# Attention of the samples joined with the preparation of the heads, ahead of the heads

## The reference, cut to what matters

```python
def _dsa_block(qb, qib, wb, posb, k_all, v_all, ki_all, topk, slopes):
    ...
    top_val, top_idx = lax.top_k(score, topk)
    k_sel = k_all[bidx, top_idx]
    v_sel = v_all[bidx, top_idx]
    logits = jnp.einsum('bqhgd,bqshd->bqhgs', qb, k_sel).astype(jnp.float32) * (HEAD_DIM_A ** -0.5)
    dist = jnp.abs(posb[None, :, None] - top_idx).astype(jnp.float32)
    logits = logits - slopes[None, None, :, :, None] * dist[:, :, None, None, :]
    ...
    p = jax.nn.softmax(logits, axis=-1).astype(v_sel.dtype)
    return jnp.einsum('bqhgs,bqshd->bqhgd', p, v_sel)
...
    k_all = jnp.concatenate([past_k.astype(x.dtype), k_a], axis=1)
    v_all = jnp.concatenate([past_v.astype(x.dtype), v_a], axis=1)
    ...
    o_a = o_a * jax.nn.silu(z_a)
```

## Time and profile before

| | us |
|---|---|
| median of 3 runs (lowest, highest) | 3160.65 (3158.35, 3172.86) |
| the profiled execution | 3176.13 |
| its span, first to last instruction | 3174.0 |
| PE busy | 2804.9 (88%) |
| DVE, ACT, POOL busy | 1156.2, 948.0, 819.6 |
| `prepare_heads`, first DMA issue to the next stage's first | 1797.16 to 1826.54 |
| `attend_samples`, the same | 2644.05 to 2727.75 |
| mean granted clock of PE, as a share of 2.4 GHz | 0.921 |

### The profile page before, as it was taken

One profiled execution on the slowest core, in us unless ns is written; L12 is line 12 of the kernel. 1 busy time (PEld: TensorE's weight loads), 2 busy tenths in 40 slices (PEclk: granted clock), 3 DMA queues, 4 the chain that ended last, 5 costly groups with the idle time before them and its releaser, 6 DMA issues. The chain is left out here.

```text
span 3174.0 us, 40095 instructions
## 1 busy us (share of the span) xinstructions
PE 2804.9 (88%) x15405; PEld 2516.8 (79%) x15429; DVE 1156.2 (36%) x2044; ACT 948.0 (30%) x1657; POOL 819.6 (26%) x713
## 2 busy tenths in 40 slices
PE   4999899999999999999999747787788785799997
PEld 3999599798998989999999736666677663587875
DVE  7000100752909044070600154566665552204142
ACT  5111111313112121121211245555556542222221
POOL 6222022111111211211122212323312320355553
PEclk6999699999999989999999877988998995699998
DMA  3222222122121212212222321222122113446453
GB/s 127 64 72 63 42 62 66 55 65 65 59 75 45 68 49 65 81 49 67 66 65 70 110 84 40 78 78 70 28 67 70 56 42 85 169 153 228 159 179 126
DMA packets 301721, 259.04 MB, mean 82 GB/s; under 512 B 88232, under 2 KB 252176, under 8 KB 299152
## 3 DMA queue, kind: packets, MB, share of 16 engines
q1 hardware_dynamic: 291564, 212.35, 23.0%
q10 hardware_dynamic: 10048, 45.27, 3.5%
HBM read 192.25 MB, written 65.33 MB: 81 GB/s over the span
## 5 line engine op out<-in xcount | busy, mean ns | idle before, releaser
L394 PE MATMUL bank<-hH,wL 128*128 128x384 f32 (+1 forms) x2928 | 981.5, 335 | 14.9 <-POOL wL L311 14.9
L395 PE MATMUL bank<-hL,wH 128*128 128x384 f32 (+1 forms) x2928 | 979.9, 335 | 0.0
L396 PE MATMUL bank<-hH,wH 128*128 128x384 f32 (+1 forms) x2928 | 979.7, 335 | 0.0
L311 POOL TENSOR_TENSOR wL<-raw,wH 128x512 fp32r<-128x512 f32 x244 | 314.2, 1288 | 1388.7 <-ACT wH L328 1388.7
L394 PEld LDWEIGHTS bank<-hH,wL 128*128 128x128 f32 (+1 forms) x2928 | 549.8, 188 | 19.2 <-issue 18.5
L395 PEld LDWEIGHTS bank<-hL,wH 128*128 128x128 f32 (+1 forms) x2928 | 549.9, 188 | 0.8
L396 PEld LDWEIGHTS bank<-hH,wH 128*128 128x128 f32 (+1 forms) x2928 | 549.8, 188 | 0.7
L328 ACT ACTIVATE wH<-raw 128x512 fp32r<-128x512 f32 x244 | 154.2, 632 | 1018.9 <-PE bank L396 963.1
L1906 POOL TENSOR_TENSOR owL<-oraw,owH 128x2048 fp32r<-128x2048 f32 x48 | 225.5, 4700 | 267.7 <-ACT owH L1926 267.7
L506 DVE TENSOR_SCALAR score<-relued,w_idx 128x512 f32<-128x512 f32 (+3 forms) x10 | 7.8, 778 | 683.4 <-ACT relued L353 683.0
L1965 PE MATMUL ob<-owH,mL 128*128 128x512 f32 x576 | 227.0, 394 | 28.6 <-POOL owL L1906 28.6
(11 more groups left out here) (302 smaller groups left out, 3521.0 us busy)
## 6 DMA issues: line engine op xcount, KB each, us to landing
raw<-in_w_in SPq DMA_DIRECT2D x240, 256.0 KB, 2.8
oraw<-in_w_out SPq DMA_DIRECT2D x48, 1024.0 KB, 5.1
proj_scratch<-ptbuf ACTq DMA_DIRECT2D x60, 576.0 KB, 2.8
xc<-proj_scratch SPq DMA_DIRECT2D x8, 1536.0 KB, 7.6
mraw<-mix_scratch SPq DMA_DIRECT2D x12, 768.0 KB, 6.1
x<-in_x_prompt SPq DMA_DIRECT2D x8, 1024.0 KB, 4.9
out_y_prompt<-yv ACTq DMA_DIRECT2D x8, 1024.0 KB, 4.4
ox<-in_x_prompt SPq DMA_DIRECT2D x8, 768.0 KB, 6.8
```

The costliest lines, as they stand in the source:

```text
L311: pool.tensor_tensor(wL[c % 2][:, :, :], raw[c][:, :, :], wH[c % 2][:, :, :].bitcast(F32), ALU.subtract).then_inc(low_ready, 1)
L394: pe.matmul(o, low, hH[:, kk, tok], start=first, stop=False)
L395: pe.matmul(o, high, hL[:, kk, tok], start=False, stop=False)
L396: last = pe.matmul(o, high, hH[:, kk, tok], start=False, stop=end)
```

## The change

`attend_samples` is gone as a stage; its programs are written into `prepare_heads`, now `prepare_and_attend`, ahead of the heads. The instructions of the tables and of the units are the old ones. What differs:

- PSUM: one bank `gate_bank` holds gates and sums; four banks `turn_bank` serve in turn the convolution rows, the nine tiles of `kvT` and the eight turns of cached keys, and then two of them the logits and two the turned probabilities; two banks hold the products; one `out_bank` holds the turned results, so that a result may be turned only when the gate of the unit before is done.
- The tiles of `kvT` are turned from the last (the samples') to the first.
- SP: behind `kvT` come all loads of the samples, `zs` now ahead of the values; then, when the nine tiles are copied, the two stores of the samples' new keys and values, a wait for both, the load `vnew`, the two stores of the prompt, and only then the heads' keys, the masks and `gnw`.
- PE: the cached keys are turned behind `kvT` and ahead of the sums of the gates. ACT and DVE do the samples' work behind all work of the preparation.

```diff
-def prepare_heads(nc, io, scratch, keep, ident, done_with):
+def prepare_and_attend(nc, io, scratch, keep, ident, done_with):
...
+        gate_bank = ctx.enter_context(nc.psum_tensor("gate_bank", [P, 512], F32))
+        turn_bank = [ctx.enter_context(nc.psum_tensor(f"turn_bank{i}", [P, 512], F32)) for i in range(4)]
+        vbank = [ctx.enter_context(nc.psum_tensor(f"value_bank{i}", [P, P], F32)) for i in range(2)]
+        obank = ctx.enter_context(nc.psum_tensor("out_bank", [P, P], F32))
+        lbank, tbank = turn_bank[0:2], turn_bank[2:4]
...
                 sp.dma_start(kvT[:, :, :], proj[C_K:C_Z, :].rearrange("(n p) t -> p n t", p=P)).then_inc(kv_loaded, 16)
+                sp.dma_start(kn[:, :, :, :], io["cache_k"]...).then_inc(cache_loaded, 16)
+                for k in range(KV):
+                    for b in range(DEC_B):
...
+                        sp.dma_start(qs[:, k, b, :, :], ...).then_inc(q_loaded, 16)
+                    sp.dma_start(kT[:, k, :, PAST:], ...).then_inc(q_loaded, 16)
+                sp.dma_start(smask[:, :], scratch["sample_mask"]).then_inc(q_loaded, 16)
+                sp.dma_start(zs[:, :, :], ...).then_inc(z_loaded, 16)
+                sp.dma_start(vn[:, :, :, :], io["cache_v"]...).then_inc(v_loaded, 16)
+                sp.wait_ge(moved, TILES)
...
+                    sp.dma_start(io[name + "_sample"]..., flat[:, NT, c:c + 2 * P]).then_inc(stored, 16)
+                sp.wait_ge(stored, 32)
+                sp.dma_start(vnew[:, :, :], io["new_v_sample"]...).then_inc(v_loaded, 16)
...
+                    sp.dma_start(io[name + "_prompt"]..., flat[:, 0:NT, c:c + 2 * P]).then_inc(stored, 16)
                 sp.dma_start(K["kT"][:, :, :], ...).then_inc(loaded, 16)
...
+                def bank_free(n):
+                    if n >= CACHE_AT + 4:
+                        pe.wait_ge(s_moved, n - CACHE_AT - 3)
+                    elif n >= KV_AT + 4:
+                        pe.wait_ge(moved, n - KV_AT - 3)
+                    elif n >= 4:
+                        pe.wait_ge(rows_out, n - 3)
...
-                for t in range(TILES):
-                    if t >= 4:
-                        pe.wait_ge(moved, t - 3)
+                for t in range(TILES - 1, -1, -1):
+                    done = TILES - 1 - t
+                    bank_free(KV_AT + done)
...
                 def turn_out(i):
                     pe.wait_ge(on_ready, i + 1)
-                    if i >= 2:
-                        pe.wait_ge(mixed, i - 1)
-                    pe.transpose(bank[6 + i % 2][:, 0:P], oN[i % 2][:, :], ident[:, :]).then_inc(on_turned, 1)
+                    if i:
+                        pe.wait_ge(mixed, i)
+                    pe.transpose(obank[:, :], oN[i % 2][:, :], ident[:, :]).then_inc(on_turned, 1)
...
-            prepare_heads(nc, io, scratch, keep, ident, done_with)
+            prepare_and_attend(nc, io, scratch, keep, ident, done_with)
             run_heads(nc, io, scratch, keep, ident)
-            attend_samples(nc, io, scratch, keep, ident)
         project_out(nc, io, scratch)
```

More of the change, by code:

```diff
@@ L528, in sem @@
             return ctx.enter_context(nc.semaphore(name))
-        proj = scratch["proj"]
+        proj, mix = scratch["proj"], scratch["mix"]
         kvT = sbt("kvT", [P, 4, TOK])
@@ L549, in prepare_heads @@
             sem, ["gate_loaded", "kv_loaded", "rows_loaded", "rows_turned", "rows_out", "summed", "drained"])
[L550 to L553, removed]
+        G, K = keep["gates"], keep
+        segcol = K["segcol"]
@@ new lines, in prepare_and_attend @@
+        PAIRS = DEC_B // 2
+        UNITS = KV * PAIRS
+        SLICES = ((0, P), (P, P), (2 * P, DEC_T))
+        qs = sbt("qs", [P, KV, DEC_B, GROUP, DEC_T])
+        zs = sbt("zs", [P, H, P])
+        kn = sbt("kn", [P, DEC_B, 2, KV * P])
+        kT = sbt("kTs", [P, KV, DEC_B, LS])
+        vn = sbt("vns", [P, DEC_B, 2, KV * P])
+        vnew = sbt("vnew", [DEC_T, DEC_B, KV * P])
+        smask = sbt("smask", [P, LS], BF16)
+        rsel = sbt("rsel", [P, PAIRS, P], BF16)
+        row = sbt("row", [P, LS], mybir.dt.int32)
@@ L654, in _, with logits @@
                 pe.matmul(segp, ones[:, :], gseg[:, :, :], start=True, stop=True).then_inc(summed, 1)
+                pe.wait_ge(q_loaded, 16 * (KV * (DEC_B + 1) + 1))
+                pe.wait_ge(s_tabled, 2)
+                pe.wait_ge(s_moved, UNITS)
+                def logits(i):
+                    k, pair = divmod(i, PAIRS)
+                    if i >= 2:
+                        pe.wait_ge(lg_ready, i - 1)
+                    o = lbank[i % 2]
+                    pe.matmul(o[:, 0:LS], rsel[:, pair, :], smask[:, :], start=True, stop=False, skip_group_check=True)
+                    for j in range(2):
+                        b = 2 * pair + j
+                        last = pe.matmul(o[j * 64:(j + 1) * 64, 0:LS], qs[:, k, b, :, :].rearrange("p g t -> p (g t)"), kT[:, k, b, :],
+                                         start=False, stop=True, skip_group_check=True)
+                    last.then_inc(lg_done, 1)
@@ new lines, in turn_out @@
+                def turn_out(i):
+                    pe.wait_ge(on_ready, i + 1)
+                    if i:
+                        pe.wait_ge(mixed, i)
+                    pe.transpose(obank[:, :], oN[i % 2][:, :], ident[:, :]).then_inc(on_turned, 1)
+                logits(0)
+                for i in range(UNITS):
+                    k, pair = divmod(i, PAIRS)
+                    if i + 1 < UNITS:
+                        logits(i + 1)
+                    pe.wait_ge(exp_ready, i + 1)
+                    if i >= 2:
+                        pe.wait_ge(p_ready, i - 1)
+                    for n, (c, w) in enumerate(SLICES):
+                        last = pe.transpose(tbank[i % 2][0:w, n * P:(n + 1) * P], lg[i % 2][:, c:c + w], ident[:, :])
+                    last.then_inc(p_turned, 1)
+                    if i:
+                        turn_out(i - 1)
+                    pe.wait_ge(p_ready, i + 1)
+                    if i == 0:
+                        pe.wait_ge(v_loaded, 32)
+                    if i >= 2:
+                        pe.wait_ge(on_ready, i - 1)
+                    for j in range(2):
+                        b = 2 * pair + j
+                        for n, (c, w) in enumerate(SLICES):
+                            v = vn[:, b, n, k * P:(k + 1) * P] if n < 2 else vnew[:, b, k * P:(k + 1) * P]
+                            last = pe.matmul(vbank[i % 2][j * 64:(j + 1) * 64, :], pT[i % 2][0:w, n, j * 64:(j + 1) * 64], v,
+                                             start=(n == 0), stop=(n == 2))
+                    last.then_inc(pv_done, 1)
@@ L656, in _ @@
+                turn_out(UNITS - 1)
             @block.scalar
@@ L666, in _ @@
                     act.wait_ge(rows_turned, half + 1)
[L667 to L670, removed]
+                    nc.scalar.activation(K["cw"][:, half * 3 * H // 2:(half + 1) * 3 * H // 2, :], turn_bank[half][:, 0:3 * H // 2 * ROWS].rearrange("p (n c) -> p n c", c=ROWS), ACT.Copy).then_inc(rows_out, 1)
+                for t in range(TILES - 1, -1, -1):
+                    done = TILES - 1 - t
+                    act.wait_ge(turned, done + 2)
+                    nc.scalar.activation(kvN[:, t, :, :], turn_bank[(KV_AT + done) % 4][:, :].rearrange("p (n c) -> p n c", n=4), ACT.Copy).then_inc(moved, 1)
+                for i in range(UNITS):
+                    k, pair = divmod(i, PAIRS)
+                    act.wait_ge(s_turned, i + 1)
+                    nc.scalar.activation(kT[:, k, 2 * pair:2 * pair + 2, 0:PAST], turn_bank[(CACHE_AT + i) % 4][:, :].rearrange("d (b s) -> d b s", b=2), ACT.Copy).then_inc(s_moved, 1)
                 act.wait_ge(stepped, 16)
@@ new lines, in _ @@
+                sample_chain(V.tensor_copy(col[:, 3:4], pcol[:, :]))
+                sample_chain(V.tensor_tensor(col[:, 1:2], col[:, 3:4], col[:, 0:1], ALU.subtract))
+                sample_chain(V.tensor_copy(rowf[:, :], row[:, :]))
+                sample_chain(V.tensor_scalar(rowf[:, :], rowf[:, :], col[:, 1:2], None, ALU.add))
+                sample_chain(V.scalar_tensor_tensor(out=rowf[:, :], in0=rowf[:, :], scalar=-1.0, in1=rowf[:, :], op0=ALU.mult, op1=ALU.min))
+                for k in range(KV):
+                    sample_chain(V.tensor_scalar(alibi[:, k, :], rowf[:, :], col[:, 2:3], 2.0 ** (-8.0 * k * GROUP / H), ALU.mult, ALU.mult))
@@ new lines, in _ @@
+                add(0)
+                dve.wait_ge(silued, 1)
+                for i in range(UNITS):
+                    if i + 1 < UNITS:
+                        add(i + 1)
+                    if i:
+                        gate(i - 1)
+                    dve.wait_ge(exp_ready, i + 1)
+                    V.reciprocal(am[:, i, 3:4], am[:, i, 2:3]).then_inc(inv_ready, 1)
+                    dve.wait_ge(inv_ready, i + 1)
+                    dve.wait_ge(pv_done, i + 1)
```

(2 more changed lines are left out.)

287 lines of the change are left out of this document (94 added, 193 removed).

## The result

The kernel after took 3155.04 us in the median of 20 runs (3135.77 to 3164.25). Beside it, on the same chip, the kernel before took 3175.07 us in 20 runs (3158.35 to 3184.45). The ratio is 0.9941, 95% interval 0.9929 to 0.9954: by it 18.7 us are saved, 0.6%, with an interval of 14.6 to 22.5 (the two medians lie 20.0 apart). The prediction said 20.7 us less and named 3140.

What follows compares the result with a forecast made beforehand. Bound by stages each closed before the next, preparation and sample attention together 113.1 us. Joined, one chain of loads, units and store takes 92.4: -20.7 us, 3176.13 to 3155.4, less 15.5 for the runs' median: 3140, range 3128 to 3156.

Steps and rivals of the forecast that it cites:

- Keys: Cached keys' load behind kvT on SP's queue: landed at u 19.2 (u: us after the joined stage's first DMA).
- Queries: Query loads and key transposes, 9.8 us from the keys' landing: logits can begin at u 29.0.
- rival C: Back-pressure on SP's issue queue: 18 small loads stall, values issued 23.6 us later; +2.9 us, 3164; chance 0.06.
- Values: Cached values' load behind zs on SP's queue: issued at u 28.4, landed at u 38.8.
- The new wait: Samples' new keys and values stored, then vnew loaded: stores 0.7 us (bound 6.0), vnew there at u 41.8.
- rival B: Loads overlap less: keys 2.7 us and stores 5.3 us more; -12.7 us, 3148; chance 0.15.
- Units: Eight two-sample attention units: 47.3 us as before, to u 89.1; single output bank costs nothing (bound 3.4 us).
- Rival D: Units run at full PE clock: at most 21.8 us more saved, -42.5 us, 3118; chance 0.05.
- Close: Store's landing and closing of the joined stage: 3.3 us as before, ending at u 92.4.
- The second chain: Key transposes, gate sums, DVE's tables and silu beside the loads: ready at u 39.5, 2.3 us before vnew.
- rival A: Vector chain, not the loads, is last: units start at u 39.5; -23.0 us, 3138; chance 0.14.
- The heads and the last stage at nothing: Stages after the joined one start as before, behind a closed stage with the same data: no cost.

Runs made afterwards that it cites:

- the early store: Kernel after, but ACT issues the two sample stores once the samples' tile is copied and SP loads vnew ahead of the values: 3151.3 us, ratio 0.9897.

## Why the prediction was right or wrong, point by point

1. *Keys.* Forecast u 19.2. PE turned them from u 19.6, with no wait of its own.
2. *Queries.* Logits forecast at u 29.0, found at u 29.3. Back-pressure (rival C) was there: the 16 loads took 22.5 us to issue (1800.69 to 1823.15), some 7.3 more than before (from the first to the last issue 21.9 us for 14.6). But the keys themselves landed 16.3 us after their issue for 8.4, 7.9 more. So the issue ends a like time behind the keys' landing, and the 9.8 us read from the old stage already held the stall. The rival charged it a second time.
3. *Values.* Forecast issued at u 28.4, landed at 38.8; found 28.0, and 10.1 us later 38.1.
4. *The new wait.* vnew issued at u 38.7 (39.5), and PE released by it at u 41.5 (41.8). The bound of 6.0 us (rival B) did not come, and the early store puts the price of the wait near 1.8 us; then the values are late next.
5. *Units.* 47.26 us for 47.3, clock 0.50. The single output bank costs nothing: periods of 6.25 to 6.29 us, and 4.84 for the last, in which no logits are issued. Rival D was wrong for this kernel, but the clock could have been had: wide logits show it.
6. *Close.* 3.66 us for 3.3. Stage 92.46 for 92.4. So close a fit is partly luck: in the second profiled execution of the same kernel vnew was issued at u 40.2, the first product came at u 43.1, and the stage took 94.05.
7. *The second chain* was mis-sized: forecast ready at u 39.5, found at u 36.6 (ACT's copy of the turned probabilities ends at 1833.52). The term most out is the 6.5 us of key transposes, 3.71 here: PE came to them straight from the transposes of kvT, and the window around them shows the full clock, where before it was 0.50 just ahead of them.

```profile
1814.89:1823.89 9.00, 6.35 (x57) 6.00 (x55) 1.94 (x6) 8.97 (x21) 0.39 (x4) 1.00 0.70 70
```

   With that, DVE's sample tables end at u 32.2, 2.7 sooner than the sum had them. The last link was another than summed: ACT's silu, which the sum puts behind those tables, waited for the load of zs until u 32.1.

```profile
1829.01 1.06 ACT L819 ACTIVATE zs<-zs 128x1024 f32<-128x1024 f32 x1 [2.12 <-DMA zs<-proj_scratch]
```

   This left rival A further off than I said and cost the sum nothing.
8. *The heads and the last stage at nothing.* The heads took +0.39. The last stage took +2.2: its products ran at half clock (0.63 us each) for 5.25 us after PE's start, where those of before did for 2.7 (2743.99 to 2746.69). The second profiled execution of the same kernel had 445.54 there, so it is scatter and not the change. PE in the kernel after, then in the kernel before, and that second execution's window:

```profile
2723.89 0.76 PE L1951 MATMUL ob<-owH,mL 128*128 128x512 f32 x1 [20.50 <-POOL owL L1892]
...
2728.71 0.63 PE L1953 MATMUL ob<-owH,mH 128*128 128x512 f32 x1
2729.14 0.57 PE L1951 MATMUL ob<-owH,mL 128*128 128x512 f32 x1
2729.55 0.40 PE L1952 MATMUL ob<-owL,mH 128*128 128x512 f32 x1
```

```profile
2743.99 0.77 PE L1965 MATMUL ob<-owH,mL 128*128 128x512 f32 x1 [19.92 <-POOL owL L1906]
...
2746.69 0.53 PE L1965 MATMUL ob<-owH,mL 128*128 128x512 f32 x1
```

```profile
2710.26:3155.80 445.54, 398.37 (x1728) 326.42 (x1728) 122.48 (x93) 110.22 (x69) 225.50 (x48) 0.95 0.51 179
```

9. *The step that failed* is the last term, the level, and not the mechanism: "The median of the runs is 3160.65, 15.5 us lower, and I apply the same difference there: 3140." The sum against the profiled execution gave 3155.4; that of the kernel after took 3157.69, and the median of 20 runs is 3155.04. The three runs shown of before lay 14.4 us below the 20 runs of it (3175.07), which stand within 1.1 us of the profiled 3176.13. So the 15.5 us subtracted were 1.1 us when measured over 20 runs: the profile stood for the kernel, and the three runs did not. Two of the three proved to be the lowest of all 20. That is bad luck, but the spread of the runs, 3158 to 3173, was on view and nearly as wide as the offset: a median of three from it could not carry 15 us.

Runs far from the median differ in the clock. Of the 20 runs of the kernel after, the two quickest (3135.77 and 3139.97) had a mean granted clock of 0.933 and 0.935, the slowest (3164.25) 0.923, and the rest lie between 0.923 and 0.932, though not in strict order (3162.48, the second slowest, has 0.928). Over all profiled executions the unchanged heads took 809 to 822 us, in no order that follows the stage ahead of them. Why the clock is granted more in one execution than in another is open.

## What to carry to other kernels

Joining two stages is worth the work that comes to lie beside a chain of loads, and a forecast read from that chain, load by load, can hold to a microsecond or two; the level to subtract it from needs as many runs as the effect is small. For effects of a few us, compare stage lengths in the traces, and times only over many runs. A small transfer issued behind big ones stalled the engine that issued it, so it belongs on a queue with nothing urgent behind it; and where PE stays at half clock though it is busy, try its kinds of product one by one: here wider logits raised the clock, while wider products with the values and filled gaps did not.

## What the runs showed of the hardware that was not expected

- The clock of the units went with the width of the logits products: 0.50 through the units in all seven profiled executions of a joined stage with 64 weight columns (five kernels), at up to 50.00 of 50.37 us busy, and at 1.00 for most of the units in all five with 128, zeros included. It did not always hold: with the filling ahead of the first unit it fell back twice. Neither the products with the values nor the filling products in bf16 made such a difference at 128 columns, so width alone is not the rule. Why the logits count and the others not is open.
- Two logits products of 64 columns into the two halves of the output partitions take less time together: their four instructions 1.18 us at half clock, those of 128 columns 2.02. The products with the values of 64 columns, which follow each other in one half, save little (1.11 for 1.22), so it looks like an overlap of the halves. The Trainium skill (TensorE: Matmul & The Clock Gate, "Why this matters for your kernels") advises such placing for products with few weight columns. The trace agrees on the product (1.18 for 2.02) and not on the stage: at 1.08 us each group and a full clock around it, the stage with the wide form is 14 us shorter over its eight units.
- Behind the big loads, eight loads of 32 KB took 16.80 us to issue on SP, the first of them alone 9.31; the median of all sixteen stayed at 0.51, as before. On ACT sixteen took 26.61 us, with a median of 1.18. On SP the delay reached only the loads behind them; on ACT it held up copies, and PE for 17.12 us.
